# Output and down projections with one 512-column moving operand for the high and low part of x

## What is computed

```
x = x + mlstm(rmsnorm(x)) @ a_w_out          # layer 0, output projection: 1024 -> 1024
x = x + (silu(gate) * val) @ f_w_down[0]     # gate, val: conv of rmsnorm(x) @ f_w_up[0]; 2816 -> 1024
k, v = shared_kv(x)
x = x + dilated_attention(x, k, v) @ b_w_out # layer 1, output projection: 1024 -> 1024
x = x + (silu(gate) * val) @ f_w_down[1]     # 2816 -> 1024
out = rmsnorm(x)
```

## Time and profile before

| | |
|---|---|
| median of 3 runs | 805.54 us (804.18 to 806.45) |
| profiled execution | 804.01 us |
| its span | 802.0 us |
| mean granted PE clock | 0.988 of full |
| PE busy | 768.8 us (96%), 6550 matmuls |
| PE weight loads busy | 753.5 us (94%) |
| DVE busy | 469.2 us (58%) |
| ACT busy | 458.9 us (57%) |
| POOL busy | 432.3 us (54%) |
| DMA | 137.26 MB, mean 171 GB/s |

### The profile page before, as it was taken

One profiled execution on the slowest core, in us unless ns is written; L12 is line 12 of the kernel. 1 busy time (PEld: TensorE's weight loads), 2 busy tenths in 40 slices (PEclk: granted clock), 3 DMA queues, 4 the chain that ended last, 5 costly groups with the idle time before them and its releaser, 6 DMA issues.

```text
span 802.0 us, 17242 instructions
## 1 busy us (share of the span) xinstructions
PE 768.8 (96%) x6550; PEld 753.5 (94%) x6550; DVE 469.2 (58%) x905; ACT 458.9 (57%) x603; POOL 432.3 (54%) x346
## 2 busy tenths in 40 slices
PE   7999989999999999989999999999899999999994
PEld 6989989999999999989999999999899999999994
DVE  5766858767677344446435544635557767676333
ACT  6543547665666456358647737746756665665441
POOL 2843446666556667652563554452255666556851
PEclk9999989999999999999999999999999999999997
DMA  9634425646565456864676486476415756554721
GB/s 293 199 114 149 159 94 169 206 163 209 185 198 181 158 188 200 226 225 94 177 228 144 143 210 143 145 209 186 117 53 161 248 171 207 180 194 138 232 96 52
DMA packets 135612, 137.26 MB, mean 171 GB/s; under 512 B 3521, under 2 KB 134932, under 8 KB 135572
## 3 DMA queue, kind: packets, MB, share of 16 engines
q1 hardware_dynamic: 127808, 130.03, 49.8%
q10 hardware_dynamic: 7764, 6.67, 6.4%
HBM read 135.57 MB, written 1.12 MB: 170 GB/s over the span
## 4 chain that ended last, share of the span: by engine, by line
PE 77%; DVE 10%; ACT 5%; issue 4%; DMA 3%; DVEq 0%; ACTq 0%; SPq 0%
PE bank L1284 12%; PE bank L1286 12%; PE bank L1285 12%; PE banks L1284 8%; PE banks L1286 8%; PE banks L1285 8%; PE bank L1504 3%; PE banks L1570 3%; PE bank L1506 3%; PE bank L1505 3%; PE banks L1536 2%; PE banks L1551 2%; DVE wlo L832 2%; DMA raw<-in_w_kv 2%; ACT whi L487 2%
## 5 line engine op out<-in xcount | busy, mean ns | idle before, releaser
L448 POOL TENSOR_TENSOR wlo<-raw,whi 128x512 fp32r<-128x512 f32 (+1 forms) x325 | 423.4, 1337 | 335.0 <-ACT whi L487 334.8
L487 ACT ACTIVATE whi<-raw 128x2048 fp32r<-128x2048 f32 (+1 forms) x136 | 238.0, 1751 | 206.7 <-PE bank L1286 97.4
L1284 PE MATMUL bank<-xsA,whi 128*128 128x256 f32 x568 | 158.7, 279 | 6.7 <-DVE wlo L907 3.0
L1286 PE MATMUL bank<-xsA,wlo 128*128 128x256 f32 x568 | 157.0, 276 | 0.0
L1285 PE MATMUL bank<-xsA,whi 128*128 128x256 f32 x568 | 156.9, 276 | 0.0
L1284 PE MATMUL bank<-xsB,whi 128*128 128x256 f32 x480 | 134.3, 280 | 0.8 <-DVE X L897 0.3
L1286 PE MATMUL bank<-xsB,wlo 128*128 128x256 f32 x480 | 132.7, 276 | 0.0
L1285 PE MATMUL bank<-xsB,whi 128*128 128x256 f32 x480 | 132.6, 276 | 0.0
L832 DVE TENSOR_TENSOR wlo<-raw,whi 128x1024 fp32r<-128x1024 f32 x83 | 106.2, 1316 | 18.7 <-ACT whi L487 18.2
L1284 PEld LDWEIGHTS bank<-xsA,whi 128*128 128x128 f32 x568 | 106.6, 188 | 8.2 <-issue 3.8
L1285 PEld LDWEIGHTS bank<-xsA,whi 128*128 128x128 f32 x568 | 106.7, 188 | 0.1
(11 more groups left out here) (200 smaller groups left out, 1630.4 us busy)
## 6 DMA issues: line engine op xcount, KB each, us to landing
raw<-in_f_w_up SPq DMA_DIRECT2D x44, 1024.0 KB, 5.1
raw<-in_w_kv SPq DMA_DIRECT2D x24, 1024.0 KB, 5.4
raw<-in_f_w_down SPq DMA_DIRECT2D x16, 1024.0 KB, 5.2
raw<-in_b_w_q SPq DMA_DIRECT2D x12, 1024.0 KB, 5.2
raw<-in_a_w_in SPq DMA_DIRECT2D x10, 1024.0 KB, 5.6
raw<-in_f_w_down SPq DMA_DIRECT2D x8, 768.0 KB, 4.9
Bi<-bias_by_distance ACTq DMA_DIRECT2D x16, 384.0 KB, 6.2
raw<-in_a_w_out SPq DMA_DIRECT2D x4, 1024.0 KB, 5.3
```

What stands on the lines that cost most here:

```text
L448: o = g.tensor_tensor(wlo[s][:, ka:kb, :], raw[s][:, ka * CW:kb * CW] .rearrange("p (k c) -> p k c", c=CW), whi[s][:, ka:kb, :].bitcast(F3 ...
L487: o = a.activation(whi[s][:, k0:k1, :], raw[s][:, k0 * CW:k1 * CW] .rearrange("p (k c) -> p k c", c=CW), ACT.Copy)
L1284: t_.matmul(ps, hi_w, hi_x, start=first, stop=False)
L1286: return t_.matmul(ps, lo_w, hi_x, start=False, stop=last)
```

## The change

In the four projections named, the high and the low part of x are one moving operand of 512 columns, so that a product is two matmuls with two weight loads instead of three with three; the bank then holds two sums (columns 0 to 255, and 256 to 511), and `residual` adds them to X in two instructions, the second after the first. All other products keep `three`.

```diff
-            def residual(k, c, m, n, b, i=0, step=0):
+            def residual(k, c, m, n, b, q, i=0, step=0, dq=0):
 
                 complete(c, m, n, i, step)
                 xk = X[:, bass.ds(k, 1), :].rearrange("p a t -> p (a t)")
-                v.tensor_tensor(xk, xk, bank[b][:, 0:S], ALU.add).then_inc(x_new, 1)
+                v.tensor_tensor(xk, xk, bank[b][:, 0:S], ALU.add).then_inc(x_half, 1)
+                dve.wait_ge(x_half, q + i * dq + (1 - KD))
+                v.tensor_tensor(xk, xk, bank[b][:, S:2 * S], ALU.add).then_inc(x_new, 1)
...
+            def both(b, hi_w, lo_w, x, first, last):
+
+                t_.matmul(bank[b][:, :], hi_w, x.rearrange("p a t -> p (a t)"), start=first,
+                          stop=False)
+                return t_.matmul(bank[b][:, 0:S], lo_w, x[:, 0, :], start=False, stop=last)
...
+                    elif wide:
+                        mm = both(banks[c], whi[s][:, kk, cs], wlo[s][:, kk, cs], xs[:, k, :, :],
+                                  first, last)
...
                         pe.wait_ge(hlo_done, p0 + ks[1] // 2)
-                        unit(u_down + j, hs, [4, 5], i, 3, ks, KF,
+                        unit(u_down + j, hs, [4, 5], i, 3, ks, KF, wide=True,
...
                             cs = slice(c * P, (c + 1) * P)
-                            three(bank[c][:, 0:S], whi[s][:, k, cs], wlo[s][:, k, cs],
-                                  aTs[:, k, 0, :], aTs[:, k, 1, :], k == 0, False)
+                            both(c, whi[s][:, k, cs], wlo[s][:, k, cs], aTs[:, k, :, :], k == 0,
+                                 False)
```

More of the change, by code:

```diff
@@ L234, in build @@
         ev_done = sem("ev_done")
-        x_new = sem("x_new")
+        x_half, x_new = sem("x_half"), sem("x_new")
         sq_done = sem("sq_done")
@@ L1051, in outproj @@
                     for c in range(2):
-                        residual(2 * u + c, c, t0 + u, u0 + u, banks[u][c])
+                        residual(2 * u + c, c, t0 + u, u0 + u, banks[u][c], q0 + 2 * u + c)
                     if u == 1:
@@ L1128, in column @@
                     for c in range(2):
-                        residual(i * 2 + c, c, i + t_down, n + 2, 4 + c, ii, step)
+                        residual(i * 2 + c, c, i + t_down, n + 2, 4 + c, q0 + m + c, ii, step,
+                                 0 if last else 2)
                     if not last:
@@ L1286, in three @@
                 return t_.matmul(ps, lo_w, hi_x, start=False, stop=last)
+            def both(b, hi_w, lo_w, x, first, last):
+                t_.matmul(bank[b][:, :], hi_w, x.rearrange("p a t -> p (a t)"), start=first,
+                          stop=False)
+                return t_.matmul(bank[b][:, 0:S], lo_w, x[:, 0, :], start=False, stop=last)
             def unit(n, xs, banks, i=0, step=0, ks=(0, KD), ktot=KD, wait_bank=(), k_wait=None,
-                     part=None, token_major=False):
+                     part=None, token_major=False, wide=False):
                 s = n % RING
@@ L1441, in outproj @@
                 if not begun:
-                    unit(u0, xs, banks[0], k_wait=k_wait, part=(0, HEAD_K))
+                    unit(u0, xs, banks[0], k_wait=k_wait, part=(0, HEAD_K), wide=True)
                 pe.wait_ge(ev_done, e0)
[L1445 to L1450, removed]
+                unit(u0 + 1, xs, banks[1], part=(0, HEAD_K), wide=True)
+                unit(u0, xs, banks[0], k_wait=k_wait, part=(HEAD_K, KD), wide=True)
+                unit(u0 + 1, xs, banks[1], part=(HEAD_K, KD), wide=True)
+                unit(u0 + 2, xs, banks[2], wide=True)
+                unit(u0 + 3, xs, banks[3], wide=True, wait_bank=[(x_new, q0 - KD + c + 1) for c in range(2)])
             def ffn(u_up, f0, u_down, p0, xs, x0, q0, s):
```

## The result

| | before | changed |
|---|---|---|
| median of 4 runs each | 804.86 us (803.63 to 806.45) | 816.48 us (814.8 to 817.66) |
| profiled execution, its span | 804.01 us, 802.0 us | 814.8 us, 812.8 us |
| mean granted PE clock | 0.988 | 0.985 (in the four runs 0.985, 0.985, 0.983, 0.982) |

A forecast was written before the change was run, and what follows sets the result against it. The prediction took PE's matmuls, paced by weight loads, to bound the kernel, with DVE pacing around the output projections. Terms -4.0 + 0.88 + 2.4 + 1.1 = +0.4 us gave a median of 805.9, range 802.7 to 809.0.

The forecast's parts named there:

- Matmuls: Down projections: a wide and narrow pair takes 0.329 us against 0.3404, over 352 products -4.0 us (2.4 to 7.0 gained).
- I take 2 ns on the wide one for its start: Projection products: the 512-column matmul takes 0.2153 us, 2 ns over the 0.2133 of its columns.
- My bounds (nothing to 7 ns): Wide matmul's start: price estimated between nothing and the 7 ns by which the old pace is over the columns.
- the pace as a weight load: Narrow matmuls: a weight load of about 0.1135 us, beside the matmul before it, sets the pace, slightly longer than 256 columns.
- saves nothing: Rival, all projections: a wide matmul costs two narrow ones, 0.227 us; only adds are left, +4.8 us, about 810.3; chance 0.12.
- Ends of the down projections: Last half's extra add lies on the path at each layer's down projection end: +0.44 us each, together +0.88.
- Output projection, layer 0: Extra adds on a full DVE delay the last addition to X and PE's resumption after the taps: +2.4 us.
- PE's lead of 0.2 us: Output projection, layer 0: unit 0's faster products start the following chains 0.2 us earlier, taken off the added time.
- Output projection, layer 1: Extra adds, partly given back as weights' low parts run into POOL's pause: +1.1 us.
- my bounds of 2.0 to 5.0: Output projections of both layers together: added time between 2.0 and 5.0 us, taken as 3.5.
- the longer wait costs the clock: Rival, output projections: PE waits 2.6 us before the second up pair, half clock costs 2.9, about 808.8; chance 0.16.
- Sum: Whole kernel: all terms give +0.4 us on the profiled 804.01, so 804.4, or 805.9 on the median.

The follow-up runs named there:

- e2: Changed kernel with the low weights' matmul 512 columns wide too, so both matmuls of a product are wide: 858.27 us in one run.
- e5: Kernel before, down projections alone changed to two matmuls of 384 columns per product (sums not those of the reference): 809.18 us in one run.
- e11: Kernel before, down projections with two equal-width matmuls per product, 512 to 128 columns by unit, whole weights: 112 ns per matmul at 128 columns, 207 at 448.
- e6: Kernel before, three narrow matmuls kept, but in the down projections only 64 of 128 weight columns loaded: 804.47 us in one run.
- e12: Kernel before, down projections with two equal-width matmuls per product, 512 to 128 columns by unit, 64 of 128 weight columns loaded: 61 ns at 128 columns.
- e9: Kernel before with wide matmuls and the second add in the two output projections alone: 809.64 us, ratio 1.0042.
- e1: Changed kernel with each wide matmul split into two narrow ones, both sums and both adds kept: 811.0 us, ratio 1.0085.
- e8: Changed kernel without the second add, so high weights x low x is left out of X: 809.57 us, ratio 1.0059.
- e7: Kernel before, down projections alone wide, issued as two wide matmuls, then two narrow ones: 805.82 us in one run.
- e13: Kernel before, down projections with two equal-width matmuls per product, 240 to 272 columns by unit, whole weights: 113 or 120 ns at 256 columns.
- e3: Kernel before with the second and third matmul of each product of three exchanged: 804.69 us, ratio 0.9995.

## Why the prediction was wrong, step by step

*Matmuls: the step that failed.* I took the pair as 0.2153 + 0.1135 = 0.329 and got -4.0 us; it takes 0.2333 + 0.120 = 0.353, which is +4.7 us for 352 products (13 ns each), and the marks show +2.3 in each layer. Two readings fell. First "I take 2 ns on the wide one for its start": it costs 20 ns over its columns. My bounds (nothing to 7 ns) came from the narrow matmul's price, on the thought that a price per instruction can't grow with the width; e2, e5 and e11 show that it does (12 ns at 320 columns, 17 at 384, 18 at 512). Second, the pace as a weight load: rows 4 are one, and hold to about 240 columns, but e6 leaves the 256 columns' 0.1133 untouched. Having the narrow matmul behind a wide one lose 7 ns as well (0.120) was in no bound. The Trainium skill (TensorE: Matmul & The Clock Gate, Back-to-back issue gap) was as far off in the same direction: its formula for an isolated matmul gives 215.8 ns at 512 columns, the traces show 231 to 233, and no stretch comes near the 131 ns that it gives as sustained.

*The rival "saves nothing"* had the right mechanism and too low a price: it put the wide matmul at 0.227, twice the narrow one, and left the narrow one behind it at 0.1135. Both are dearer than that, so the down projections lose time rather than keep it. I gave it 0.12 because the half-clock matmuls show no overhead. That is true of them and says nothing of full clock: that comparison was the argument that misled me. It could not even tell the load from the columns. PE in e11 at half clock, 224 columns on whole weights, eight starts in 1.70 us:

```profile
775.67 0.41 PE L1303 MATMUL banks<-hs,wlo 128*128 128x224 f32 x1
...
777.37 0.41 PE L1303 MATMUL banks<-hs,wlo 128*128 128x224 f32 x1
```

That is 0.213 each, as 256 columns take, where the same columns on half the weights take 0.187 in e12 at half clock, 224 / 1.2 GHz. At 1.2 GHz the whole load alone thus holds 0.213, and 256 columns need the same.

*Ends of the down projections.* Predicted 0.88; measured 0.46 at the program's end and 0.3 in layer 0, where PE's matmul at k = 7 starts 0.74 us behind the one before it and not 0.32. The mechanism was right.

*Output projection, layer 0.* Predicted +2.4; the marks give +1.8, but at the same length of the stretch at 105 it is some +3. The mechanism held at each place: adds on a full DVE, ACT behind the last one, the taps, PE waiting. The sizes: from unit 1's first add to the last addition to X the change costs 2.74 us (12.10 before, 14.84 now), where I had 2.62; the wlo pieces took 0.94 more, not 0.3, and the low part at 131.53 gave back 0.51 besides the idle 0.32. PE's lead of 0.2 us was no lead: in e9, with the long stretch as before, unit 1's first add comes 0.25 us later behind PE's first matmul than before. It came 0.64 earlier in the changed kernel (120.89 against 121.53) because of the short stretch. That the marks' +1.8 lies near my +2.4 is partly luck.

*Output projection, layer 1.* Predicted +1.1; measured +0.1 (e1 and e9 have 0.4; the ten profiles with the old output projections and 3.4 us of half clock there span 0.7 us among themselves). DVE's timeline there, and POOL's:

```profile
607.65 2.82 DVE L832 TENSOR_TENSOR wlo<-raw,whi 128x1024 fp32r<-128x1024 f32 x2
610.39 0.47 DVE L848 SCALAR_TENSOR_TENSOR xsB<-X,vcols,xsB 128x256 fp32r<-128x256 f32 x1
```
```profile
602.82 5.43 POOL L448 TENSOR_TENSOR wlo<-raw,whi 128x512 fp32r<-128x512 f32 x4 [9.60 <-ACT whi L487]
610.47 5.67 POOL L448 TENSOR_TENSOR wlo<-raw,whi 128x512 fp32r<-128x512 f32 x4 [2.22 <-ACT whi L487]
```

The shift put the weights' low part into POOL's pause (2.82 us against 3.56), as foreseen, and the low part of x behind it too: 0.47 where it had 1.51, which I had not counted. POOL's pause had grown, too, from 0.71 us to 2.22. That one us is the miss, and the wait for the taps that I saw growing to 2.5 us in this layer stayed where it was (1.15 us, 1.22 before). At equal clock both layers together cost some 3.1 us, inside my bounds of 2.0 to 5.0. The Trainium skill (SBUF — State Buffer, SBUF: two separate sides) has a VectorE instruction with two SBUF inputs and a GpSimd instruction that reads SBUF exclude each other, the first to start holding the port to its end. The trace agrees: the adds, with one input in PSUM, keep 0.41 to 0.42 wherever they stand; the low parts take 0.47 to 0.48 alone, 0.87 to 1.52 where one of POOL's instructions had begun before them, and 0.47 to 0.48 in the four cases where they began just before it, as at 610.39.

*The rival "the longer wait costs the clock"* came true beside the first. I expected a wait of 2.6 us and 2.9 us lost; it was 2.16 us and 1.6 lost, and e1, e8 and e9 tie it to the adds through the wait. The other new stretch, 1.6 us at 359, belongs to no part of the change.

*Sum.* Predicted -4.0 + 0.88 + 2.4 + 1.1 = +0.4. Measured in the span: matmuls +4.7, ends +0.75, output projections +3.0 and +0.1, clock +1.6 through the change, and by the execution +1.6 at 359 and -1.1 at 106, and 0.2 ahead of it all: +10.8. Of the miss of 10.4, 8.7 is the one term, the matmuls, and most of that the wide one. At the old pace, too, the change loses, as e1 shows: its adds stand where others already waited for DVE.

What stays open: why the price over the columns grows from 7 ns at 256 to some 18 at 512, since no run separates the read of the moving operand from the write of the bank; what makes a stretch of 256 columns settle at 0.1133 or at 0.120; and what decides, in a given execution, whether a wait of two microseconds costs the clock, and for how long. No version with a wide matmul beats the kernel before: e7 comes nearest with 805.82 in a single run, against a median of 804.59.

## What to carry to other kernels

Fewer and wider instructions save only what the instruction count costs, so measure that before trading: vary the width alone, and the weight load alone, and see which of them moves the pace. Where two limits lie within a few ns of each other, as the load (0.113) and 256 columns (0.107 and a price) here, a pace equal to one of them doesn't show that it is the limit. Work that is moved to an engine which others wait for can be paid in full, and with it whatever the longer wait does to TensorE's clock: 2.6 us of adds cost some 3 us in layer 0 and nearly nothing in layer 1, where they moved DVE's other work out of POOL's way. And two single traces are compared only after their clocks: look in each stage for stretches at half clock that one has and the other has not.

## What the runs showed of the hardware

- A matmul of 512 fp32r columns with its own weight load takes 231 ns from start to start at full clock, 18 over its columns (e2; 233 before a narrow one); 256 columns take 113.3, 7 over. At half clock the 256 columns take 0.213 us, with nothing on top.
- A load of 128x128 weights holds the pace at 0.112 us for 128 columns at full clock (e11) and at 0.213 for 224 columns at half clock (e11); with 64 weight columns the same matmuls go at 0.061 and 0.187 (e12).
- 256 columns don't always go at 0.1133: behind a wide matmul they take 0.116 to 0.120, behind a wait the first ones do, and in three of seven stretches of e13 all of them take 0.120.
- Loading the same weights twice in a row is neither cheaper nor dearer than other weights each time (0.1133 in e3 as in the kernel before).
- The fall of the clock is no fixed function of the wait: behind 2.15 us at the taps it came in 3 of 3 profiles, behind a wait for KT of 2 us or more in 10 of 15, behind 1.4 to 1.6 us at the taps in none of 13; but in e12's down projection it came behind waits of 1.79 us (at 760.34) and of 1.52 us (at 750.78, with another of 0.94 us two microseconds earlier). A stretch costs some 1.6 us, as much as 14 matmuls of 256 columns.
- Behind the same wait of 3.62 us half clock lasted 3.4 us in ten profiles and 6.8 us in six. That alone moves a stage here by 1.1 us or more from one execution to the next.
